# Causal masks of three attentions: from bf16 matmuls into PSUM to a VectorE add-and-reduce that writes the scores to SBUF

## The chip, the cores and the metric

The kernel runs on one core of a Trainium2 chip. The metric is the device time of one execution in microseconds; the median of three executions of the kernel before is 2026.19 us.

## What is computed

One sequence of 256 tokens with 1024 features goes through two networks one after the other, all in float32. The first has two layers; each is a SwiGLU feed-forward network (width 2816), a hybrid mixer, and a second feed-forward network. The mixer holds a gated linear recurrence, a convolution branch, and a latent attention with 8 heads. The second network is a dilated attention with 16 heads and three groups, a feed-forward network, a "forgetting" attention with 16 heads, another feed-forward network and a final norm.

What the change touches is the middle of each of the three attentions, shown here for the latent one (`mla_branch` of the reference):

```python
sc = (jnp.einsum('bqhd,bkhd->bhqk', qn, k_nope, preferred_element_type=jnp.float32)
      + jnp.einsum('bqhr,bkr->bhqk', qp, k_pe, preferred_element_type=jnp.float32)) * scale
mask = key_idx[None, :] <= q_idx[:, None]
sc = jnp.where(mask, sc, jnp.finfo(jnp.float32).min)
p = jax.nn.softmax(sc, axis=-1).astype(v.dtype)
return jnp.einsum('bhqk,bkhd->bqhd', p, v)
```

The dilated attention masks each group with a band, the forgetting attention uses the causal mask again.

## The kernel before

All weights come from HBM as 326 slots of 128 x 2048 floats (1 MB each), through a ring of three buffers. For each slot SyncE issues the load into `raw`, ScalarE rounds it to `whi` (`split`, line 586), VectorE computes the rest `wlo` = raw - whi (line 1107), and TensorE multiplies three times: activations high by `whi`, high by `wlo`, low by `whi` (`use`, line 1946, and `down_block`, line 1997). A slot is 24 matmuls of 512 columns. The order of every engine's work is written out by hand; semaphores connect the engines, and each engine works its own list in order.

The three attentions lie between or inside these slots.

- **Latent attention** (`scores_of` in `mix`, lines 2275 and 2276; twice, once for each layer). 8 heads in four pairs. `scores_of(p)` runs four score products (two heads, two row blocks of 128 queries with 128 and 256 keys). VectorE takes row maxima (`largest`, line 1390), ScalarE does the exponentials (line 778) and a scaling (line 786), TensorE transposes the probabilities (`turn_p`, line 2285) and multiplies by V (`pv`, line 2297). Between these steps stand whole stretches of projections, and VectorE also runs the 31 taps of the convolution branch (`conv`, line 1330) and the biased projections (line 1341).
- **Dilated attention** (`dil`). 32 items in 16 pairs, each with 512 score columns: `scores_of` (lines 2412 and 2415) puts two items into two PSUM banks. `largest` (line 1581), `exp` (line 962), `normed` (lines 1593 and 1595), `turn_p` (line 2422), `pv` (line 2436). A pair's `turn_p` comes a slot and more after its scores.
- **Forgetting attention** (`attention`, used by `fox`). 16 heads, with nothing else on TensorE for most of it. In iteration `h` TensorE does the scores of head `h` (`qk`, lines 2121 and 2123), the products by V of head `h-4` (`pv`, line 2152) and the transpositions of head `h-2` (`turn_p`, line 2133). VectorE takes the maxima (line 1211), ScalarE the exponentials (line 656) and the copy of the transposed probabilities (line 647).

Every score product opens with a mask matmul: the stationary operand is the bf16 identity `identb`, the moving one a piece of the bf16 masks `maskb`; it writes the mask into PSUM, and the float32 score product adds to it. GpSimd makes `identb` and `maskb` at the start (`masks`, line 1903).

```python
pe.matmul(dst[:, cols], identb[:], masks[rb][:, cols], start=True, stop=False)            # 2121
signal(dve.reduce_max(negmax[...], scores(groups, h, rb), AX, negate=True), max_done, ...)  # 1211
act.wait_ge(max_done, item(b, groups, h, rb))                                             # 653
if h >= h0 + 2:
    act.wait_ge(p_turned, item(b, groups, h - 2, rb))
act.activation(p_rows[h % 2][rb], scores(groups, h, rb), ACT.Exp, bias=negmax[...], accum_out=den[...])
```

`p_rows` are two SBUF buffers (heads `h % 2`), so ScalarE waits until TensorE has transposed head `h-2` before it writes head `h` there. `qk(h)` waits for `exp_done` of head `h-2`, `turn_p(h-2)` for `exp_done` of `h-2` and the copy of `h-4`, `pv(h-4)` for the copy of `h-4`. On ScalarE the order is exponentials of `h`, copy of `h-2`. VectorE also has `o_out` after head 11 (lines 1199 and 1204).

Of the kernel before, what the change touches and what calls it, by code (L numbers as in the profile page):

```python
# [26 lines left out]
AX = mybir.AxisListType.X  # L27
# [190 lines left out]
def program(nc, w_stream, gains, vecs, gate_w, chunks, b_f, fins, consts, x_in, positions, out):  # L218
    ctx = ExitStack()
    with ctx:  # L220
# [17 lines left out]
        identb = sb("identb", [P, P], BF16)  # L238
        maskb = sb("maskb", [P, 2 * P + RB * W], BF16)
# [14 lines left out]
        ident = con_("ident")  # L254
# [54 lines left out]
        d_p = [region(8960 + W * n, W) for n in range(2)]  # L309
# [28 lines left out]
        masks_done, trig_act, trig_pool = sem("masks_done"), sem("trig_act"), sem("trig_pool")  # L338
# [240 lines left out]
        def _(act):  # L579
# [57 lines left out]
            def attention(b, heads, h0, groups, p_rows, p_cols, tail=lambda h: None):  # L637

                lag = buffers(groups)
# [83 lines left out]
            def mix(b):  # L723
# [48 lines left out]
                def exp(p):  # L772
                    for h in (2 * p, 2 * p + 1):
                        act.wait_ge(mla_max, M * MH + h + 1)
                        if p:
                            act.wait_ge(mla_turned, M * MH + h - 1)
                        for rb in range(RB):
                            ins = act.activation(pm[h % 2][rb], mla_scores(h, rb), ACT.Exp, bias=negmax[:, 2 * h + rb:2 * h + rb + 1],
                                                 accum_out=den[:, rb * NH + h:rb * NH + h + 1])
# [144 lines left out]
            def dil(b):  # L924
# [33 lines left out]
                def exp(i):  # L958
                    act.wait_ge(max_done, b.head * 2 + i + 1)
                    if i >= 2:  # L960
                        act.wait_ge(p_turned, b.head * 2 + i - 1)
                    act.activation(d_p[i % 2], bank(dil_bank(i)), ACT.Exp, bias=negmax[:, i:i + 1],
# [49 lines left out]
            def fox(b):  # L1012
# [48 lines left out]
                attention(b, NH, 0, 1, x_p, x_pt, tail=lambda h: first_o(h - (NH - 2)))  # L1061
# [38 lines left out]
        def _(dve):  # L1100
# [37 lines left out]

            def copy_turn(b, plan, name, dst, parts):
# [42 lines left out]
            def attention(b, heads, h0, groups, p_cols, o_rows, more=lambda h: None):  # L1182
# [1620 lines left out]
```

## Time and profile before

| | |
|---|---|
| timed executions | 2026.12, 2026.19, 2026.45 us |
| profiled execution, first to last instruction (span) | 2024.2 us |
| TensorE matmul busy | 2001.7 us (99%) |
| TensorE weight load busy | 1649.0 us (81%) |
| VectorE busy | 1221.0 us (60%) |
| ScalarE busy | 1025.0 us (51%) |
| GpSimd busy | 284.7 us (14%) |
| mask matmuls recorded | 81 (32 latent, 17 dilated, 32 forgetting), with 96 loads of `identb` |

The page gives the profiled execution's span and no separate time for it; the timed median stands 2.0 us above the span, which is what lies around the first and last instruction. Matmuls are pipelined and their ends are modelled, so that their durations overlap: what one costs is the distance from its start to the next start, or its length in the chain of work. Some matmul records are missing: of the dilated attention's 32 mask matmuls 17 have one, while all 32 loads of the identity do.

### The profile page before, as it was taken

The page shows a single profiled execution, that of the slowest core. Times are in us where ns is not written, and L with a number is a line of the kernel's source. Part 1 is how long each engine was busy: PE and PEld are TensorE (multiplying, and loading weights), DVE is VectorE, ACT ScalarE, POOL GpSimd, SP SyncE. Part 2 cuts the span into 40 slices and gives each one's busy share as a digit, 9 for nine tenths or more (in the row PEclk, how much of TensorE's full clock was granted, in tenths as well). Part 3 has the DMA queues.
Part 4 walks back from the last instruction along what each step waited for, and adds up shares of the span by engine and source line. Part 5 has one row for each costly group of instructions (what it writes and reads, how often), then busy time and mean ns, then how long its engine had stood idle before and what let it go on. Part 6 is the DMA issues. An engine that isn't in the chain of part 4 may idle for free.

```text
span 2024.2 us, 26360 instructions
## 1 busy us (share of the span) xinstructions
PE 2001.7 (99%) x9813; PEld 1649.0 (81%) x9828; DVE 1221.0 (60%) x1374; ACT 1025.0 (51%) x1318; POOL 284.7 (14%) x365
## 2 busy tenths in 40 slices
PE   8999999999999999999999999999999999999998
PEld 6888888788888888887788888787778888788886
DVE  5555798865555555898855555555555555545554
ACT  5444685744445445586654445544444445455443
POOL 1000469200000000568100002111100000000000
PEclk9999999999999999999999999999999999999999
DMA  7554554445555554554455544344335554415552
GB/s 269 195 186 173 178 199 168 173 178 187 186 187 200 186 186 178 172 211 165 175 179 197 189 173 169 144 146 142 129 125 193 188 188 174 171 65 200 188 189 96
DMA packets 54626, 354.15 MB, mean 175 GB/s; under 512 B 7696, under 2 KB 8336, under 8 KB 12816
## 3 DMA queue, kind: packets, MB, share of 16 engines
q1 hardware_dynamic: 53968, 352.51, 49.1%
q8 instruction: 53, 0.87, 0.2%
q10 hardware_dynamic: 576, 0.53, 0.1%
q14 instruction: 29, 0.24, 0.0%
HBM read 351.97 MB, written 1.05 MB: 174 GB/s over the span
## 4 chain that ended last, share of the span: by engine, by line
PE 91%; DVE 5%; ACT 2%; issue 1%; DVEq 1%; DMA 0%; SPq 0%; POOLq 0%; ACTq 0%; POOL 0%
PE psum L1946 64%; PE psum L1997 18%; DVE wlo L1107 3%; PE psum L2075 2%; PE psum L2012 1%; PE psum L2415 1%; PE psum L2436 1%; PE psum L1958 1%; PE psum L2422 1%; ACT whi L586 1%; PE psum L2123 0%; PE psum L2152 0%; DMA raw<-w_stream 0%; DVE psum L1330 0%; PE psum L2276 0%
## 5 line engine op out<-in xcount | busy, mean ns | idle before, releaser
L1107 DVE TENSOR_TENSOR wlo<-raw,whi 128x2048 fp32r<-128x2048 f32 x325 | 752.0, 2317 | 388.5 <-ACT whi L586 386.0
L1946 PE MATMUL psum<-whi,xTh 128*128 128x512 f32 (+1 forms) x1920 | 764.3, 398 | 2.5 <-DVE xTl L1124 1.8
L1946 PE MATMUL psum<-whi,xTl 128*128 128x512 f32 (+1 forms) x1920 | 745.9, 388 | 0.0
L1946 PE MATMUL psum<-wlo,xTh 128*128 128x512 f32 (+1 forms) x1920 | 745.7, 388 | 0.0
L586 ACT ACTIVATE whi<-raw 128x2048 fp32r<-128x2048 f32 x325 | 622.0, 1916 | 239.8 <-PE psum L1997 151.3
L1946 PEld LDWEIGHTS psum<-whi,xTh 128*128 128x128 f32 x1920 | 361.2, 188 | 79.5 <-issue 7.1
L1946 PEld LDWEIGHTS psum<-whi,xTl 128*128 128x128 f32 x1920 | 361.1, 188 | 76.0
L1946 PEld LDWEIGHTS psum<-wlo,xTh 128*128 128x128 f32 x1920 | 361.7, 188 | 68.1
L1997 PE MATMUL psum<-whi,braT 128*128 128x512 f32 x1056 | 337.8, 390 | 0.0
L1997 PEld LDWEIGHTS psum<-whi,braT 128*128 128x128 f32 x1056 | 198.2, 188 | 41.2
L1997 PE MATMUL psum<-wlo,braT 128*128 128x512 f32 x528 | 205.5, 389 | 0.0
L683 ACT ACTIVATE arena<-psum,small 128x256 f32<-128x256 f32 x132 | 55.4, 471 | 194.8 <-PE psum L1946 194.7
L688 ACT ACTIVATE braT<-psum 128x256 fp32r<-128x256 f32 x132 | 43.4, 382 | 217.3 <-PE psum L2012 217.3
L1250 DVE TENSOR_TENSOR braT<-psum,braT 128x256 fp32r<-128x256 f32 x132 | 49.9, 420 | 112.1 <-ACT braT L688 112.1
L1997 PEld LDWEIGHTS psum<-wlo,braT 128*128 128x128 f32 x528 | 99.1, 188 | 20.0
L1243 DVE SCALAR_TENSOR_TENSOR arena<-psum,small,arena 128x256 f32<-128x256 f32 x132 | 57.8, 480 | 85.0 <-ACT arena L683 84.6
L1794 POOL TENSOR_SCALAR arena<-arena,vec 128x256 f32<-128x256 f32 x60 | 83.9, 1399 | 0.3 <-issue 0.3
L1330 DVE SCALAR_TENSOR_TENSOR psum<-arena,vec,psum 128x256 f32<-128x256 f32 x174 | 73.8, 485 | 5.4 <-issue 0.4
L1743 POOL TENSOR_SCALAR small<-small 128x2 f32<-128x2 f32 x9 | 1.7, 191 | 502.0 <-ACT arena L613 502.0
L1797 POOL TENSOR_TENSOR arena<-arena 128x256 f32<-128x256 f32 x60 | 68.0, 1134 | 8.8
L605 ACT ACTIVATE xTh<-psum,gain 128x256 fp32r<-128x256 f32 x80 | 31.3, 474 | 63.0 <-PE psum L1958 62.5
L1946 PE MATMUL psum<-whi,braT 128*128 128x512 f32 x160 | 56.0, 410 | 2.1 <-issue 2.1
(260 smaller groups left out, 1467.6 us busy)
## 6 DMA issues: line engine op xcount, KB each, us to landing
raw<-w_stream SPq DMA_DIRECT2D x326, 1024.0 KB, 4.8
bias<-chunks SPq DMA_DIRECT2D x18, 256.0 KB, 5.1
x<-x_in SPq DMA_DIRECT2D x2, 512.0 KB, 5.6
raw<-w_stream SPq DMA_DIRECT2D x4, 256.0 KB, 7.1
arena<-gate_w SPq DMA_DIRECT2D x2, 512.0 KB, 5.2
arena<-fins SPq DMA_DIRECT2D x2, 512.0 KB, 5.5
con<-consts SPq DMA_DIRECT2D x1, 720.0 KB, 10.8
out<-x ACTq DMA_DIRECT2D x2, 256.0 KB, 2.3
```

What stands on the lines that cost most here:

```text
L586: act.activation(whi[:, r], raw[:, r], ACT.Copy).then_inc(hi_done, 1)
L683: act.activation(f_sg[:, rb], gate_up(b, j)[:, rb, 0:256], ACT.Silu, scale=rs[:, rb:rb + 1]).then_inc(silu_done, 1)
L688: act.activation(h_of(b, j, 0)[:, :, rb * P:(rb + 1) * P], psum[:, 6 + rb, 0:256].rearrange("p (t s) -> p t s", s=P), ACT.Copy).then_inc(t ...
L1107: TT(wlo[:, r], raw[:, r], whi[:, r].bitcast(F32), ALU.subtract).then_inc(lo_done, 1)
L1243: ins = STT(f_h[:, rb], gate_up(b, j)[:, rb, 256:512], rs[:, rb:rb + 1], f_sg[:, rb], ALU.mult, ALU.mult)
L1250: TT(h_of(b, j, 1)[:, :, rows], psum[:, 6 + rb, 0:256].rearrange("p (t s) -> p t s", s=P), h_of(b, j, 0)[:, :, rows].bitcast(F32), ALU.sub ...
L1330: ins = STT(cacc[:, t] if k == TAPS - 1 else acc, cpad[:, t, k:k + S], w, acc, ALU.mult, ALU.add)
L1794: TS(ctap[:, k % 2], window, w, None, ALU.mult)
L1797: ins = TT(cacc[:, CONV_DVE], cacc[:, CONV_DVE], ctap[:, k % 2], ALU.add)
L1946: ins = pe.matmul(dst(rb), s(kt)[:, rows], w[:, r, at_:at_ + cols], start=start and n == 0 and k == 0, stop=stop and n == len(kts) - 1 and ...
L1997: ins = pe.matmul(pair(c)[:, rb], s[:, t, rows], w[:, r, t * D + c * W:t * D + (c + 1) * W], start=start and t == 0 and k == 0, stop=stop ...
L2075: ins = pe.transpose(dst[0:rows.shape[1], col:col + P], rows, ident)
```

## The change

The mask matmuls go. VectorE's row maximum becomes `tensor_tensor_reduce`: it reads the scores from PSUM and the float32 mask from SBUF (`con`, where the constants lie already), writes (scores + mask) x -1 to the SBUF buffer of the probabilities, and reduces with a minimum, which gives the negated maximum. ScalarE's exponential then runs in place in SBUF with scale -1. The wait for the buffer moves from ScalarE to VectorE. The dilated attention gets four such buffers for two. `identb`, `maskb`, their semaphore and GpSimd's `masks` are dropped.

```diff
-        d_p = [region(8960 + W * n, W) for n in range(2)]
+        d_p = [region(at_, W) for at_ in (8960, 9472, 11008, 11520)]
...
                         act.wait_ge(max_done, item(b, groups, h, rb))
-                        if h >= h0 + 2:
-                            act.wait_ge(p_turned, item(b, groups, h - 2, rb))
-                        signal(act.activation(p_rows[h % 2][rb], scores(groups, h, rb), ACT.Exp, bias=negmax[:, 2 * h + rb:2 * h + rb + 1],
-                                              accum_out=den[:, rb * NH + h:rb * NH + h + 1]), exp_done, groups, rb)
+                        signal(act.activation(p_rows[h % 2][rb], p_rows[h % 2][rb], ACT.Exp, bias=negmax[:, 2 * h + rb:2 * h + rb + 1],
+                                              scale=-1.0, accum_out=den[:, rb * NH + h:rb * NH + h + 1]), exp_done, groups, rb)
...
+            def masked_max(rows, scores_, mask, at_):
+
+                return dve.tensor_tensor_reduce(rows, scores_, mask, -1.0, 3.0e38, ALU.add, ALU.min, negmax[:, at_:at_ + 1])
...
                         dve.wait_ge(s_in, item(b, groups, h, rb))
-                        signal(dve.reduce_max(negmax[:, 2 * h + rb:2 * h + rb + 1], scores(groups, h, rb), AX, negate=True),
-                               max_done, groups, rb)
+                        if h >= h0 + 2:
+                            dve.wait_ge(p_turned, item(b, groups, h - 2, rb))
+                        signal(masked_max(p_rows[h % 2][rb], scores(groups, h, rb), masks[rb], 2 * h + rb), max_done, groups, rb)
...
                         dve.wait_ge(mla_s, M * MH + h + 1)
+                        if p:
+                            dve.wait_ge(mla_turned, M * MH + h - 1)
                         for rb in range(RB):
-                            ins = dve.reduce_max(negmax[:, 2 * h + rb:2 * h + rb + 1], mla_scores(h, rb), AX, negate=True)
+                            ins = masked_max(pm[h % 2][rb], mla_scores(h, rb), causal[:, (1 - rb) * P:2 * P], 2 * h + rb)
                         ins.then_inc(mla_max, 1)
...
                     dve.wait_ge(s_in, b.head * 2 + i + 1)
-                    dve.reduce_max(negmax[:, i:i + 1], bank(dil_bank(i)), AX, negate=True).then_inc(max_done, 1)
+                    if i >= 4:
+                        dve.wait_ge(p_turned, b.head * 2 + i - 3)
+                    blk = dil_item(i)[1]
+                    masked_max(d_p[i % 4], bank(dil_bank(i)), con_("mask_d")[:, blk * W:(blk + 1) * W], i).then_inc(max_done, 1)
...
-                        pe.matmul(dst[:, cols], identb[:], masks[rb][:, cols], start=True, stop=False)
                         for g in gs:
                             ins = pe.matmul(dst[:, g * keys:(g + 1) * keys], q_of(h, g)[:, rb * P:(rb + 1) * P],
-                                            k_of(h, g)[:, 0:keys], start=False, stop=g == gs[-1])
+                                            k_of(h, g)[:, 0:keys], start=g == g0, stop=g == gs[-1])
...
-                                pe.matmul(dst, identb[:], maskb[:, (1 - rb) * P:2 * P], start=True, stop=False)
-                                ins = pe.matmul(dst, qT[0:QK, h, rb * P:(rb + 1) * P], kT[0:QK, h, 0:keys], start=False, stop=True)
+                                ins = pe.matmul(dst, qT[0:QK, h, rb * P:(rb + 1) * P], kT[0:QK, h, 0:keys], start=True, stop=True)
...
-                    for bank_ in banks:
-                        pe.matmul(bank_, identb[:], maskb[:, 2 * P + blk * W:2 * P + (blk + 1) * W], start=True, stop=False)
```

The order of the built program shows what the diff does not. VectorE, forgetting attention, the maxima of heads 3 and 4 among the calls before (`small` holds the maxima):

```order
L1211 TENSOR_REDUCE small<-psum 128x1 [waits scores_in_psum] x4
L1690 TENSOR_SCALAR arena<-psum,small 128x512 [waits slot_used]
L1690 TENSOR_SCALAR arena<-psum,small 128x512
L1211 TENSOR_REDUCE small<-psum 128x1 [waits scores_in_psum] x20
L1199 RECIPROCAL small<-small 128x8 [waits exp_done]
```

and the same place now (`arena` is the probabilities' buffer, `con` the mask):

```order
L1693 TENSOR_SCALAR arena<-psum,small 128x512
L1133 ISA arena,small<-psum,con 128x128 [waits p_turned,scores_in_psum]
L1133 ISA small 128x1
L1133 ISA arena,small<-psum,con 128x256 [waits p_turned,scores_in_psum]
L1133 ISA small 128x1
L1133 ISA arena,small<-psum,con 128x128 [waits p_turned,scores_in_psum]
L1133 ISA small 128x1
```

Each maximum has become two instructions, the second of which only writes the 128 x 1 result, and from head 2 on they also wait for `p_turned`. VectorE's list has 96 such pairs for 96 reductions.

TensorE, one iteration of the forgetting attention before:

```order
L2121 MATMUL psum<-maskb,identb 128x128 [waits exp_done]
L2123 MATMUL psum<-arena 128x128
L2152 MATMUL psum<-arena 128x64 [waits pt_out_act]
L2121 MATMUL psum<-maskb,identb 128x256 [waits exp_done]
L2123 MATMUL psum<-arena 128x256
L2152 MATMUL psum<-arena 128x64 [waits pt_out_act]
L2152 MATMUL psum<-arena 128x64
L2133 MATMUL psum<-con,arena 128x128 [waits pt_out_act,exp_done] x2
L2133 MATMUL psum<-con,arena 128x128
```

Now the two rows of line 2121 are gone, the score products carry the wait for `exp_done`, and nothing else moved. The lists of ScalarE and SyncE keep their order; GpSimd's loses its two copies.

## Rows read from the trace of the kernel before

**Rows 1.** The page: busy time by engine; the chain that ended last.

```profile
PE 2001.7 (99%) x9813; PEld 1649.0 (81%) x9828; DVE 1221.0 (60%) x1374; ACT 1025.0 (51%) x1318; POOL 284.7 (14%) x365
...
PE 91%; DVE 5%; ACT 2%; issue 1%; DVEq 1%; DMA 0%; SPq 0%; POOLq 0%; ACTq 0%; POOL 0%
```

**Rows 2.** Chain, dilated attention, the mask matmuls of one pair: start us, us, what.

```profile
1265.84 0.07 issue
1265.91 0.38 PE psum L2412
```

**Rows 3.** Timeline, one pair: last normalization, first transposition (start, us, engine, line).

```profile
1331.15 0.49 DVE L1595 TENSOR_SCALAR arena<-arena,small 128x512 f32<-128x512 f32 x1
...
1336.41 0.27 PE L2422 MATMUL psum<-con,arena 128*128 128x128 f32 x1
```

**Rows 4.** Chain, mix stage of the first layer: where it leaves and rejoins TensorE.

```profile
348.21 0.62 DVE small L1390 x2
...
384.71 5.74 PE psum L1946 x24
```

**Rows 5.** Chain, forgetting attention, one head.

```profile
1787.00 0.06 PE psum L2121
1787.06 0.28 PE psum L2123 x2
1787.34 0.17 PE psum L2152 x2
1787.51 0.11 PE psum L2121
1787.62 0.43 PE psum L2123 x2
1788.05 0.39 PE psum L2152 x4
1788.44 0.34 PE psum L2133 x3
```

**Rows 6.** Timeline, the same stretch: VectorE's maxima, the next head's mask, ScalarE's exponential.

```profile
1786.31 0.62 DVE L1211 TENSOR_REDUCE small<-psum 128x1 f32<-128x128 f32 x2 [1.15 <-PE psum L2123]
...
1786.84 0.22 PE L2121 MATMUL psum<-maskb,identb 128*128 128x128 bf16 x1
...
1787.10 0.37 ACT L656 ACTIVATE arena<-psum,small 128x128 f32<-128x128 f32 x1 [0.48 <-PE psum L2133]
```

**Rows 7.** Timeline, the first heads: exponentials, copy, and TensorE behind them.

```profile
1780.34 0.37 ACT L656 ACTIVATE arena<-psum,small 128x128 f32<-128x128 f32 x1 [2.63 <-DVE small L1211]
...
1781.06 0.20 ACT L656 ACTIVATION_READ_ACCUMULATOR arena<-psum,small 128x1 f32 x1
1781.15 0.49 ACT L647 ACTIVATE arena<-psum 128x384 f32<-128x384 f32 x1
...
1781.31 0.23 PE L2121 MATMUL psum<-maskb,identb 128*128 128x128 bf16 x1 [0.55 <-ACT arena L656]
...
1781.78 0.41 PE L2152 MATMUL psum<-arena 128*128 128x64 f32 x2
```

**Rows 8.** Groups by line and shape: busy us, mean ns of one, idle before.

```profile
L1211 DVE TENSOR_REDUCE small<-psum 128x1 f32<-128x256 f32 x16 | 6.6, 415 | 0.0
L1250 DVE TENSOR_TENSOR braT<-psum,braT 128x256 fp32r<-128x256 f32 x132 | 49.9, 420 | 112.1 <-ACT braT L688 112.1
L1133 DVE TENSOR_TENSOR xTl<-psum,xTh 128x512 fp32r<-128x512 f32 x12 | 7.8, 684 | 8.2 <-ACT xTh L631 8.2
L778 ACT ACTIVATE arena<-psum,small 128x256 f32<-128x256 f32 x16 | 7.5, 471 | 0.0
L786 ACT ACTIVATE arena<-arena,small 128x256 f32<-128x256 f32 x16 | 7.9, 494 | 0.0
```

**Rows 9.** Timeline, end of the dilated attention: TensorE's longest wait there.

```profile
1477.76 0.47 PE L1946 MATMUL psum<-whi,braT 128*128 128x512 f32 x1 [2.14 <-issue]
```

**Rows 10.** Busy us by engine (TensorE, weight load, VectorE, ScalarE, GpSimd), granted clock, DMA.

```profile
1400.00:1500.00 100.00, 97.45 (x582) 76.72 (x587) 56.52 (x78) 45.68 (x72) 11.76 (x36) 0.98 0.35 125
```

More of the change, by code:

```diff
@@ L252, in vec_ @@
             return vec[:, VEC[n][0] + i:VEC[n][0] + i + m]
-        ident = con_("ident")
+        ident, causal = con_("ident"), con_("mask_s")
         at = [0]
@@ L635, in hi_turns, with attention @@
                     ins.then_inc(thi, 1)
-            def attention(b, heads, h0, groups, p_rows, p_cols, tail=lambda h: None):
-                lag = buffers(groups)
+            def attention(b, heads, h0, p_rows, p_cols, tail=lambda h: None):
+                groups, lag = 1, buffers(1)
                 def turned_out(h):
@@ L959, in exp @@
                     act.wait_ge(max_done, b.head * 2 + i + 1)
-                    if i >= 2:
-                        act.wait_ge(p_turned, b.head * 2 + i - 1)
-                    act.activation(d_p[i % 2], bank(dil_bank(i)), ACT.Exp, bias=negmax[:, i:i + 1],
+                    act.activation(d_p[i % 4], d_p[i % 4], ACT.Exp, bias=negmax[:, i:i + 1], scale=-1.0,
                                    accum_out=den[:, i:i + 1]).then_inc(exp_done, 1)
@@ L1060, in fox @@
                 first_o = lambda n: hi_turns(b, plan, f"o{n}", xTh[:, 2 * n:2 * n + 2], at_=4 + n)
-                attention(b, NH, 0, 1, x_p, x_pt, tail=lambda h: first_o(h - (NH - 2)))
+                attention(b, NH, 0, x_p, x_pt, tail=lambda h: first_o(h - (NH - 2)))
                 upto(13)
@@ L1180, in next_norm, with attention @@
                     norm_lo(b.next, 0)
-            def attention(b, heads, h0, groups, p_cols, o_rows, more=lambda h: None):
+            def attention(b, heads, h0, groups, p_rows, p_cols, o_rows, masks, more=lambda h: None):
                 lag = buffers(groups)
@@ L1402, in o_lo @@
                     TT(latT[:, 1, p], psum[:, 6, 0:S], latT[:, 0, p].bitcast(F32), ALU.subtract).then_inc(mla_lo, 1)
+                dve.wait_ge(rest_in, 48)
                 dve.wait_ge(vec_in, M * 16 + 16)
@@ L1594, in normed @@
                     dve.drain()
[L1595 removed]
+                    TS(d_p[i % 4], d_p[i % 4], rden[:, i:i + 1], None, ALU.mult).then_inc(p_normed, 1)
                 def o_lo(first):
@@ L1701, in more @@
                             lo_turns(b, plan, f"o{n}", xTl[:, 2 * n:2 * n + 2], xTh[:, 2 * n:2 * n + 2], at_=4 + n)
-                attention(b, NH, 0, 1, x_pt, x_o, more=more)
+                attention(b, NH, 0, 1, x_p, x_pt, x_o, (causal[:, P:2 * P], causal), more=more)
                 for n in range(2, 4):
@@ L1902, in _ @@
             TS(ang[:, 1], ang[:, 1], -1.0, np.pi / 2, ALU.mult, ALU.add).then_inc(trig_pool, 1)
-            def masks():
-                wait(rest_in, 48)
-                pool.tensor_copy(identb[:], ident)
-                m0 = CON["mask_s"][0]
-                pool.tensor_copy(maskb[:], con[:, m0:m0 + 2 * P + RB * W]).then_inc(masks_done, 1)
             def ffn(b):
                 rms(b)
-                if not b.early:
-                    masks()
             def fin(b):
@@ L2106, in whole, with attention @@
                         between()
-            def attention(b, heads, h0, groups, p_rows, p_cols, q_of, k_of, masks, v_of, before_pv=lambda: None):
+            def attention(b, heads, h0, groups, p_rows, p_cols, q_of, k_of, v_of, before_pv=lambda: None):
                 lag = buffers(groups)
@@ L2410, in scores_of @@
                     own = slice(blk * P, (blk + 1) * P)
-                    for bank_ in banks:
-                        pe.matmul(bank_, identb[:], maskb[:, 2 * P + blk * W:2 * P + (blk + 1) * W], start=True, stop=False)
                     for g, cols, keys in ((0, slice(0, S), slice(0, S)), (1, slice(S, S + P), own), (2, slice(S + P, W), own)):
                         for bank_, r in zip(banks, rows):
-                            ins = pe.matmul(bank_[:, cols], d_T[pair_ % 3][r, g, own], d_T[pair_ % 3][r, GROUPS + g][:, keys], start=False, stop=g == 2)
+                            ins = pe.matmul(bank_[:, cols], d_T[pair_ % 3][r, g, own], d_T[pair_ % 3][r, GROUPS + g][:, keys], start=g == 0, stop=g == 2)
                             if g == 2:
```

17 lines of the change are left out of this document (5 added, 12 removed).

## The prediction

> **What bounds the kernel.** I began with busy time by engine and then read the chain that ended last [rows 1]: TensorE is busy 99% of the span and 91% of the chain is its own work; the weight stream is nowhere in it (DMA 0%). So an instruction less on TensorE is worth its issue time, as long as no other engine's path is about to be the longer one. Three places decide, one for each attention, and the chain tells them apart. In the dilated attention every piece of the chain belongs to TensorE; the only other item is 0.07 us of issue in front of a pair's masks [rows 2]. In the forgetting attention the steady heads are TensorE's alone too, in seven pieces [rows 5]. In the mix stage it is not so: right after the third pair's scores the chain leaves TensorE for VectorE, passes through VectorE and ScalarE work, and comes back 36.5 us later [rows 4]. An average share would hide that.
>
> **The masks on TensorE.** 96 mask matmuls go, 32 in each attention. The dilated ones come in pairs (512 columns for each of two items); in the chain a pair and the gap in front are 0.07 + 0.38 = 0.45 us [rows 2]. 16 pairs x 0.45 = 7.2 us. The 0.38 us stand for both matmuls of a pair, of which mostly one has a record. The gap may stay when the 64-row score product follows the 128-row projection directly (0.38 us gained), or a second such gap behind the masks may close too (0.52 us): 6.1 to 8.3 us, and I take the middle. In the latent and the forgetting attention a head has a mask of 128 and one of 256 columns: 0.06 + 0.11 = 0.17 us [rows 5], so 16 x 0.17 = 2.7 us each if all of it were on the path.
>
> The Trainium skill ("TensorE: Matmul & The Clock Gate", Part 2) says that a weight load is pulled ahead of running matmuls when row groups do not conflict. By that rule the 64-row load behind a 128-row projection would wait for it, and the gap would stay: 6.1 us by the page against 7.2 by the row. No row shows that transition bare.
>
> **VectorE's new work.** A float32 two-input pass over 128x256 takes 420 ns where the reduction takes 415 [rows 8]: the same rate, one element a cycle, also with the result written. So the main instruction costs what the maximum did. New is the second instruction, which delivers the 128 x 1 result. VectorE's trace has none. From below it is nothing; from above it is the 0.20 us of ScalarE's accumulator read. Of that read ScalarE's next instruction waits only 0.09 us (1781.06 to 1781.15) [rows 7], and I take 0.09 us, as it is the same kind of step. A head's two maxima thus grow from 0.62 [rows 6] to 0.80 us.
>
> **ScalarE.** The exponential reads SBUF in place of PSUM: 494 against 471 ns for 128x256 [rows 8], 0.023 us more each, 0.05 us a head with the smaller one. Where ScalarE is not on the path this is free.
>
> **Dilated attention: all of it gained.** A pair has two maxima (two reads more, 0.2 us), two exponentials (0.05 us). They are covered: the last normalization ends at 1331.64 and the first transposition comes at 1336.41 [rows 3], 4.8 us of cover in which VectorE also splits a slot. Four buffers for two mean that the new wait for `p_turned` looks four items back, and is long past. -7.2 us.
>
> **Latent attention: nearly nothing.** Of the 2.7 us only the masks ahead of the point where the chain leaves TensorE count: two pairs and the start of the third, 0.34 x 2 + 0.17 = 0.85 us a layer. Behind it the chain is VectorE's, and its maxima are in it twice (third and fourth pair, 8 instructions): 8 x 0.09 = 0.7 us a layer more. The masks of the fourth pair lie beside it. Net 0.15 us a layer, and some 0.1 us more because VectorE now waits less for the third pair: -0.5 us for both layers. Bounds: -2.7 us if VectorE's wait absorbs its own growth, +1.5 us if the read costs the 0.20 us. What is late next there is the split of the slot at 384.7.
>
> **Forgetting attention: a new loop.** Here the moved wait matters. Before, VectorE took the maxima at once (1786.31) and only ScalarE waited for the transpositions of head h-2: these have been issued by 1786.84, the exponential starts at 1787.10, 0.26 us later [rows 6]. Now VectorE waits for them, and maxima and exponentials stand one behind the other. The loop over two heads, from the issue of `turn_p(h-2)` to that of `turn_p(h)`:
>
> - 0.26 us until VectorE starts [rows 6]; 0.80 us maxima; 0.05 us to ScalarE (TensorE starts 0.05 us after ScalarE's read ends at 1781.26 [rows 7]; I take the same).
> - Queued on ScalarE behind the exponentials of h is the copy for h-2, and `pv(h-2)` needs it before `turn_p(h)`. Exponential to copy 0.81 + 0.05, copy 0.49, to the product by V 0.14 (1781.64 to 1781.78) [rows 7]: 1.49 us.
> - TensorE from there: 0.17 + 0.43 + 0.39 + 0.34 = 1.33 us [rows 5].
>
> That is 3.93 us for two heads, 1.97 us a head, where the rows now sum to 0.06 + 0.28 + 0.17 + 0.11 + 0.43 + 0.39 + 0.34 = 1.78 us, with TensorE never idle. So each of the 12 heads 4 to 15 costs 0.19 us more, 2.2 us, in place of 0.17 us less. Added: once the division after head 11 (1.55 us on VectorE between two maxima that are 1.17 us apart) 0.4 us; the last head's chain, which is no longer hidden, 0.4 us; and back 0.3 us for the masks of the first two heads, which stand among projections. +2.7 us. Bounds: +1.3 us with a read that costs nothing and quick handovers, +4.5 us with the 0.20 us read.
>
> GpSimd's two copies at the start were hidden and nothing waited for them: 0.
>
> **Sum.** -7.2 - 0.5 + 2.7 = -5.0 us on a span of 2024.2 us. The timed median lies 2.0 us above the span, which the change does not touch: 2026.2 - 5.0 = 2021.2 us. The bounds of the three together give 2016.5 to 2025.7. One more term has no sign: TensorE waits 2.14 us at the end of the dilated attention [rows 9], and in that stretch the granted clock falls to 0.98 of full, that is 2% of 100 us, some 3.4 us at half of 2.4 GHz [rows 10]. Whether that recurs is worth up to 1.7 us either way.
>
> **Rivals.** About 0.2% (4.1 us) is what a measurement of this kernel can tell from no change.
>
> - *The loop stays hidden.* If handovers are short enough, all 96 masks are gained: -7.2 - 2.7 - 2.7 = -12.6, 2013.6 us. For it: TensorE never waits now. Against it: the sum above exceeds TensorE's 1.61 us a head by 0.36 us, more than any one term. Chance 0.06.
> - *The two-input reduction runs at half rate.* 256 further elements take 684 - 420 = 264 ns [rows 8], so a head's 384 elements cost 0.40 us more: the loop 0.20 us a head, 2.8 us with its ends; four heads a layer in the mix stage's chain, 3.2 us; the dilated attention's 1.1 us a pair is covered. -5.0 + 6.0 = +1.0, 2027.2 us. Against: plain two-input rows are at full rate. The Trainium skill ("Vector Engine (DVE) Microarchitecture Reference", section 7) says that an accumulating operation with two float32 SBUF sources halves its rate; here one source is PSUM, so by its letter it does not apply, and no row shows either. Chance 0.09.
> - *The dilated masks were partly cover.* If one of a pair's two masks hid the change from 128 to 64 rows, half of the 0.38 us comes back as a gap and a pair gains 0.19 us: 3.0 us in place of 7.2, which gives 2025.4 us. For it: a gap of 0.07 us already stands ahead of the masks [rows 2]. Against: nothing there waits for another engine. Chance 0.11.
> - *Slower: the new instruction has a large fixed cost.* Each x us more on one of them costs 14x in the forgetting attention (one x a head and its ends) and 16x in the mix stages. From x = 0.30 us on (30 x 0.30 = 9.1 us against 5.0 gained) the kernel is slower by over 4.1 us; at x = 0.5, 15 us: 2036 us. For it: the instruction's kind is nowhere in this trace. Against: every VectorE row with one pass is near its element count. Chance 0.06.
>
> **Numbers.** The forecast has 0.68, with a range of its own of 2018.5 to 2023.5; about three quarters of that lies below 2022.1, the rest within 0.2%. Faster: 0.52 + 0.06 = 0.58. Same: 0.16 + 0.09 + 0.11 = 0.36. Slower 0.06. The range for 8 in 10 leaves out the first rival, the last and half of the second: 2016.5 to 2026.5.
>
> **What would show it.** Right: no L2412, L2275 or L2121; in the dilated attention a pair's period shorter by 0.4 to 0.5 us; in the forgetting attention the head's period up from 1.77 to 1.9 or 2.0 us, with TensorE idle before its scores for ScalarE, and VectorE idle for the transpositions (L2133) and no more for the scores; the mix stage within 1 us of its old length. Wrong: a period there at or below 1.77 us, a maximum of 128x512 that takes over 0.9 us, a dilated pair that gains less than 0.3 us, or new waits of TensorE for `wlo`.

## The result, and the profile after

The changed kernel is slower: 2032.94 us median (2031.52 to 2036.32, 6 runs) against 2026.17 us (2024.37 to 2026.45, 6 runs), a ratio of 1.0039 with a 95% interval of 1.0029 to 1.0049, or 6.8 us more. The forecast was 2021.2 us with a range that ended at 2026.5 us, so the result lies 6.4 us above its end. The profiled execution took 2033.63 us, with a span of 2031.7 us.

The page of the kernel after: busy time by engine (as [rows 1]) and the granted clock in 40 slices.

```profile
PE 2007.0 (99%) x9732; PEld 1659.7 (82%) x9732; DVE 1222.5 (60%) x1470; ACT 1028.2 (51%) x1318; POOL 282.6 (14%) x363
...
PEclk9999999999999999999999999999999999969999
```

TensorE has 96 matmuls less to do and is busy 5.3 us longer than before. The second row says why: one slice of the clock, about 50 us wide, is a 6 among nines. Busy time by engine in five stretches of the forgetting attention (the columns are those of [rows 10]) puts it in place:

```profile
1770.00:1780.00 10.00, 8.90 (x46) 7.95 (x44) 3.53 (x18) 4.89 (x20) 0.00 (x0) 0.71 0.13 55
1780.00:1790.00 10.00, 10.00 (x45) 9.46 (x45) 1.96 (x12) 4.50 (x17) 0.00 (x0) 0.50 0.00 1
1790.00:1800.00 10.00, 10.00 (x44) 9.46 (x43) 3.43 (x16) 4.08 (x15) 0.00 (x0) 0.50 0.00 0
1800.00:1810.00 10.00, 10.00 (x45) 9.46 (x45) 2.61 (x16) 4.08 (x15) 0.00 (x0) 0.50 0.01 2
1810.00:1820.00 10.00, 10.00 (x60) 8.98 (x60) 2.85 (x6) 5.17 (x10) 0.00 (x0) 0.91 0.01 2
```

For 30 us on end TensorE is never idle (10.00 of 10 us) and its granted clock is 0.50 of full, 1.2 GHz. The shortfall of the five rows, 0.29, 0.50 three times and 0.09 of 10 us, is that of 37.6 us at half clock. TensorE's waits (who waits for whom: us in total, times, longest) have one row in the attention:

```profile
PE psum L2115 <- ACT arena L652: 1.1, 1, 1.1
```

The chain that ended last, in the same place (start us, us, what), shows what surrounds that wait and the fall behind it:

```profile
1764.12 5.47 PE psum L1940 x24
1769.62 1.01 DVE arena L1693 x2
...
1770.94 0.28 DVE arena L1133
...
1771.92 0.69 ACT arena L652 x3
...
1772.65 0.49 PE psum L2115 x2
...
1774.50 0.65 PE psum L2125 x3
1775.14 0.43 PE psum L2115 x2
1775.57 0.32 PE psum L2144 x2
1775.89 0.96 PE psum L2115 x2
...
1778.24 0.43 PE psum L2115 x2
```

The projections end; VectorE scales the second half of V (L1693), takes the maxima of head 2 (L1133), ScalarE takes the exponentials (L652), and TensorE waits for them 1.1 us in front of the scores of head 4 (L2115). About 2 us after it starts again the three transpositions (L2125) take 0.65 us where they took 0.34 [rows 5], and a head then takes 3.10 us (1775.14 to 1778.24) where it took 1.77 us. This goes on through the last scores, which end at 1807.79; the clock is full again from 1811.7 us on (0.65 in the stretch from 1811 to 1812, 1.00 in the next), 2.8 us ahead of the output projection.

Everything ahead of the attention went as forecast or a little better. One pair of the dilated attention in the chain after (beside [rows 2]):

```profile
1262.71 1.58 PE psum L1940 x6
1264.30 1.08 PE psum L2403 x12
```

In the chain the scores (L2403) follow the projection (L1940) within 0.01 us. The ends of the pieces are modelled, so the starts have to be read beside it; the timeline of the same pair, before and after (start us, us):

```profile
1265.45 0.39 PE L1946 MATMUL psum<-whi,xTl 128*128 128x512 f32 x1
1265.68 0.12 PEld L2412 LDWEIGHTS psum<-maskb,identb 128*128 128x128 bf16 x2 [0.27 <-issue]
1265.91 0.38 PE L2412 MATMUL psum<-maskb,identb 128*128 128x512 bf16 x1
1266.22 1.15 PE L2415 MATMUL psum<-arena 64*128 64x256 f32 x12
```

```profile
1263.91 0.39 PE L1940 MATMUL psum<-whi,xTl 128*128 128x512 f32 x1
1264.23 0.96 PEld L2403 LDWEIGHTS psum<-arena 64*128 64x128 f32 x12 [0.36 <-issue]
1264.23 1.15 PE L2403 MATMUL psum<-arena 64*128 64x256 f32 x12
```

From the start of the last projection to that of the scores it is 0.32 us where it was 0.77: 0.45 us gained. One projection follows another after 0.23 us, so 0.09 us still stand in front of the 64-row scores, as they did behind the masks before (1265.91 to 1266.22 is 0.31 us). By the same transitions in both chains, the stretch with the dilated attention goes from 483.57 us (1030.37 to 1513.94) to 476.46 us (1029.23 to 1505.69), 7.1 us less, and the 1.1 us between 1030.37 and 1029.23 are the gain of the two latent layers. The last transition ahead of the forgetting attention's projections for V is 8.28 us earlier (1760.17 before, 1751.89 after). When the projections for V end, the kernel after is 8.75 us ahead (1769.59 against 1778.34 in the chain before). It enters the output projection at 1814.51 where the kernel before did at 1807.35.

The new instructions, first by line and shape (busy us, mean ns | idle before), then as one line's instructions (shortest, median and longest ns, first and last start):

```profile
L1133 DVE CUSTOM_DVE_ANT_0 arena<-psum,con 128x256 f32<-128x256 f32 x32 | 13.4, 420 | 0.0
```

```profile
L1133 DVE DVE_READ_ACCUMULATOR2_ANT small<- x96: 75/82/85, 319.1 to 1809.9; 128x1 f32 x96
```

420 ns against 415 for the plain maximum of the same shape [rows 8]: full rate. And the second instruction, 82 ns long, costs nothing in a row of them: in the timeline of the run with four buffers below (start us, us; its line numbers are the same) the next one starts when the read starts, not when it ends:

```profile
1766.68 0.28 DVE L1133 CUSTOM_DVE_ANT_0 arena<-psum,con 128x128 f32<-128x128 f32 x1
...
1766.89 0.08 DVE L1133 DVE_READ_ACCUMULATOR2_ANT small<- 128x1 f32 x1
1766.89 0.42 DVE L1133 CUSTOM_DVE_ANT_0 arena<-psum,con 128x256 f32<-128x256 f32 x1
```

So the whole loss, and more, lies in 16 heads of one attention: from the end of the projections for V to the output projection 29.01 us before, 44.92 us after.

### The profile page after: what moved, and what is told of

The parts are those of the page before. It is cut to its first block, busy times and chain, and to the rows that moved or that the text cites. A ratio compares the mean times of both kernels' runs of the same rounds, so it can differ in the third digit from the quotient of the medians.

```text
span 2031.7 us, 26290 instructions
## 1 busy us (share of the span) xinstructions
PE 2007.0 (99%) x9732; PEld 1659.7 (82%) x9732; DVE 1222.5 (60%) x1470; ACT 1028.2 (51%) x1318; POOL 282.6 (14%) x363
## 4 chain that ended last, share of the span: by engine, by line
PE 89%; DVE 7%; ACT 2%; DVEq 1%; issue 1%; DMA 0%; SPq 0%; POOLq 0%; ACTq 0%
PE psum L1940 62%; PE psum L1991 18%; DVE wlo L1099 3%; PE psum L2069 1%; PE psum L2006 1%; DVE psum L1327 1%; PE psum L2115 1%; PE psum L2403 1%; PE psum L2424 1%; PE psum L1952 1%; PE psum L2144 1%; PE psum L2410 1%; ACT whi L584 1%; DVEq L1319 1%; DMA raw<-w_stream 0%
## 5 line engine op out<-in xcount | busy, mean ns | idle before, releaser
L1940 PE MATMUL psum<-whi,xTh 128*128 128x512 f32 (+1 forms) x1920 | 763.9, 398 | 4.1 <-DVE xTl L1116 3.4
L1940 PE MATMUL psum<-whi,xTl 128*128 128x512 f32 (+1 forms) x1920 | 745.5, 388 | 0.0
L1940 PE MATMUL psum<-wlo,xTh 128*128 128x512 f32 (+1 forms) x1920 | 745.4, 388 | 0.0
L1940 PEld LDWEIGHTS psum<-whi,xTh 128*128 128x128 f32 x1920 | 361.1, 188 | 80.8 <-issue 7.1
L1940 PEld LDWEIGHTS psum<-whi,xTl 128*128 128x128 f32 x1920 | 360.9, 188 | 75.9
L1940 PEld LDWEIGHTS psum<-wlo,xTh 128*128 128x128 f32 x1920 | 361.6, 188 | 68.1
L1991 PE MATMUL psum<-whi,braT 128*128 128x512 f32 x1056 | 337.8, 390 | 0.0
L1133 DVE CUSTOM_DVE_ANT_0 arena<-psum,con 128x128 f32<-128x128 f32 (+1 forms) x96 | 40.6, 465 | 53.1 <-PE psum L2125 28.2
```

Of the source, the lines that this page charges most:

```text
L1133: return dve.tensor_tensor_reduce(rows, scores_, mask, -1.0, 3.0e38, ALU.add, ALU.min, negmax[:, at_:at_ + 1])
L1940: ins = pe.matmul(dst(rb), s(kt)[:, rows], w[:, r, at_:at_ + cols], start=start and n == 0 and k == 0, stop=stop and n == len(kts) - 1 and ...
L1991: ins = pe.matmul(pair(c)[:, rb], s[:, t, rows], w[:, r, t * D + c * W:t * D + (c + 1) * W], start=start and t == 0 and k == 0, stop=stop ...
```

## The experiments

**First question: why does the clock fall?** Two theories at first. *Theory 1, content:* without the mask matmuls TensorE does too little there for the full clock. *Theory 2, wait:* VectorE now waits for the transpositions of two heads before, that delay reaches TensorE, and a microsecond of idleness drops the clock. The first four runs take the parts of the change in the forgetting attention apart: all of them back, only the mask matmuls back, only the wait away, only the mask matmuls away. In the expectations a "head period" is the time from one head's scores to the next one's, and "clock" is the mean over the span.

**The old forgetting attention with the rest of the change.**

```diff
-  signal(masked_max(p_rows[h % 2][rb], scores(groups, h, rb), masks[rb], 2 * h + rb), max_done, groups, rb)
+  signal(dve.reduce_max(negmax[:, 2 * h + rb:2 * h + rb + 1], scores(groups, h, rb), AX, negate=True), max_done, groups, rb)
...
+  pe.matmul(dst[:, cols], identb[:], masks[rb][:, cols], start=True, stop=False)
```

> The change in the dilated attention and the latent layers alone; the forgetting attention is as in the kernel before (masks by TensorE, plain row maximum, exponential out of PSUM). Both theories put the whole loss into the forgetting attention, so both expect 2026.2 - 7.2 (dilated attention) - 1.0 (two stages of the latent layers) = 2018.0 us, a head period of 1.77 us in the forgetting attention and a mean clock of 0.998. More than 2022 us would mean that a part of the loss comes from elsewhere.

Measured 2017.71 us (2017.05 to 2018.09), ratio 0.996 (0.9946 to 0.9974). The rest of the change is worth the 8.2 us that the anchors above gave, and the loss is the forgetting attention's alone.

**Masks added twice, by TensorE and by VectorE; two buffers and the moved wait stay.**

```diff
+  pe.matmul(dst[:, cols], identb[:], masks[rb][:, cols], start=True, stop=False)
   for g in gs:
       ins = pe.matmul(dst[:, g * keys:(g + 1) * keys], q_of(h, g)[:, rb * P:(rb + 1) * P],
-                      k_of(h, g)[:, 0:keys], start=g == g0, stop=g == gs[-1])
+                      k_of(h, g)[:, 0:keys], start=False, stop=g == gs[-1])
```

> The changed kernel with the mask matmuls of the forgetting attention back on TensorE, so that this mask is added twice, by TensorE and by VectorE. The moved wait on the turned exponentials stays. Theory 1 (content: without the mask matmuls TensorE does too little there for the full clock): the clock stays at 2.4 GHz, head period 1.85 to 1.95 us, 2019 to 2022 us. Theory 2 (wait: the idle microsecond from the moved wait drops the clock, whatever TensorE computes): the clock still falls to 1.2 GHz for over 30 us, head period about 3.1 us, 2033 us or more.

Measured 2019.57 us (2019.04 to 2021.41), ratio 0.9973 (0.9962 to 0.9983), clock 0.998 or 0.999 in all 8 runs. The moved wait is there and costs its time (two heads from 1771.86 to 1775.87 in its chain, 4.0 us), but the clock does not fall. TensorE's first wait in this run is 0.7 us.

**Four buffers, no masks.** VectorE waits for the turn of head h-4.

```diff
-  x_p = [[region(14464 + 384 * b + 128 * rb, (rb + 1) * P) for rb in range(RB)] for b in range(2)]
+  x_p = [[region(at_ + 128 * rb, (rb + 1) * P) for rb in range(RB)] for at_ in (14464, 14848, 18624, 19008)]
...
-  if h >= h0 + 2:
-      dve.wait_ge(p_turned, item(b, groups, h - 2, rb))
+  if h >= h0 + 4:
+      dve.wait_ge(p_turned, item(b, groups, h - 4, rb))
```

> The changed kernel with four buffers for the exponentials of the forgetting attention instead of two, so that VectorE waits for the turn of four heads before and not of two. The mask matmuls stay away. Theory 1 (content): the clock still falls, head period about 3.1 us, 2033 us. Theory 2 (wait): the clock stays at 2.4 GHz, TensorE is the bound at 1.6 to 1.7 us a head, 2015 to 2018 us.

Measured 2033.11 us (2031.65 to 2036.54), ratio 1.0038 (1.0024 to 1.0052): as slow as the change itself. Without the moved wait the clock falls all the same. Its waits have the same row as the change: 1.1 us, once.

**The kernel before without its mask matmuls in the forgetting attention.** It leaves out that attention's causal mask.

```diff
-  pe.matmul(dst[:, cols], identb[:], masks[rb][:, cols], start=True, stop=False)
```

> The kernel before, with the mask matmuls of the forgetting attention taken out and nothing in their place: it leaves out the causal mask of that attention, and moves no wait. Theory 1 (content): the clock falls there, some 13 to 15 us more than the kernel before, about 2040 us. Theory 2 (wait): no fall, 26 heads lose the 0.11 us of mask matmuls each where TensorE is the bound, about 2023.5 us.

Measured 2042.14 us (2041.49 to 2044.67), ratio 1.0085 (1.0068 to 1.0102). 32 matmuls fewer, nothing added and nothing moved, and 16 us slower. (The expectation's other sum, "26 heads" of 0.11 us, should have been 16 heads of 0.17 us, 2.7 us; it leads to the same 2023.5.) One stretch, then the row of its waits:

```profile
1790.00:1800.00 10.00, 10.00 (x43) 9.39 (x43) 1.87 (x6) 4.61 (x20) 0.00 (x0) 0.50 0.01 2
```

```profile
PE psum L2122 <- ACT arena L656: 1.0, 1, 1.0
```

All four came out as theory 1 had it; theory 2 in the form of the moved wait is out. But the waits, read in each run's profiled execution, show something that neither theory names. The three kernels without masks there have a first wait of 1.0 to 1.1 us, the two runs with them 0.5 and 0.7 us, because the masks of heads 2 and 3 stand in front of that wait and fill it. That gives **theory 3**: the length of this one wait, at the change from the projections to the attention, decides, and afterwards nothing brings the clock back.

**Second question: content or first wait?** Four runs with four buffers, in which the number and the place of the mask matmuls vary. The diff is that for heads 0 to 3; for heads 4 to 15 and for every second head its first line has `h >= 4` and `h % 2 == 1`, and for all heads the matmul stands without a condition.

```diff
+  masked = h < 4
+  if masked:
+      pe.matmul(dst[:, cols], identb[:], masks[rb][:, cols], start=True, stop=False)
```

> Four buffers for the exponentials and the mask matmuls of the forgetting attention back on TensorE (mask added twice). If the 1.9 us by which the run with masks twice and two buffers is above the run with the old forgetting attention (2019.6 against 2017.7) are the new loop through the buffers, they go: clock full, head period 1.77 us throughout, 2017.0 to 2018.3 us. If they are VectorE's longer maximum or ScalarE's longer exponential, it stays at 2019 to 2020 us.

> Four buffers; the mask matmuls on TensorE again, but only from head 4 on (heads 0 to 3 without). In all three runs that lost the clock, TensorE had waited 1.0 to 1.1 us for the first exponential just before. Theory 1 (content): the clock may fall in heads 0 to 3, and comes back within the attention once the masks are there: 2018 to 2025 us. Theory 3 (the longer first wait drops the clock and nothing in the attention brings it back): half clock until the output projection, 30 us or more, 2033 to 2038 us.

> Four buffers; the mask matmuls on TensorE again, but only for heads 0 to 3 (heads 4 to 15 without). Theory 1 (content): the clock is full through the first four heads and falls behind them, so the stretch at half clock is some 5 to 8 us shorter than the 37 us of the changed kernel: 2028 to 2031 us. Theory 3 (the longer first wait): with the first wait short again the clock never falls: 2015 to 2017 us.

> Four buffers; mask matmuls on TensorE for every second head of the forgetting attention. If half of them is enough for the full clock, this beats both kernels: 2017.7 less half of 16 x 0.17 us, 2016.3 us. If not, half clock for 35 us or more, 2032 to 2036 us.

Measured, with the first wait of the profiled execution:

| mask matmuls in | us, median | ratio, 95% | first wait | clock fell |
|---|---|---|---|---|
| all heads | 2018.13 | 0.9963 (0.995 to 0.9976) | 0.6 us | 0 of 5 |
| heads 0 to 3 | 2016.68 | 0.9954 (0.994 to 0.9968) | 0.6 us | 0 of 4 |
| every second head | 2015.53 to 2017.30; 2034.34 to 2039.35 | | 0.9 us | 3 of 12 |
| heads 4 to 15 | 2015.94 to 2018.09; 2037.01 to 2040.60 | | 1.1 us | 5 of 10 |

The third and fourth are two kernels each: in an execution the clock either falls (mean 0.986 to 0.989) or does not (0.998 or 0.999), so both groups are given and no median. Each group lies near what was expected with and without a fall; that one kernel would do both was in no expectation. The second row of the table refutes theory 1: twelve heads without a mask matmul run at full clock, 2016.7 us where theory 1 wanted 2028 to 2031. One of these heads in its chain, and the start of the next:

```profile
1775.70 0.22 PE psum L2130 x2
1775.93 0.17 PE psum L2159 x2
1776.10 0.49 PE psum L2130 x2
1776.59 0.39 PE psum L2159 x4
1776.98 0.34 PE psum L2140 x3
1777.31 0.22 PE psum L2130 x2
```

1.61 us a head, the sum of TensorE's own pieces, and no wait. The last row of the table shows the other half. Where the clock fell in heads 0 to 3, the masks that follow from head 4 on do not bring it back (the profiled execution, 0.50 in every stretch from 1775 to 1815 us), which speaks against theory 1 as well. That half of the executions escape there, where none did in the kernels with the same wait and no masks at all, shows that 1.1 us of waiting does not decide alone. With four buffers, all masks and no fall the run is 2.6 us below the one with two buffers when both stand at 0.999 (2016.7 against 2019.0 to 2019.6): 12 heads of 0.2 us, the price of the loop.

**Third question: the first wait by itself.** Four runs that change it in both directions. (a) All mask matmuls on TensorE, first wait longer:

```diff
+  TS(x_v[:, rb, W:W + 256], pair(units.place("v1"))[:, rb, 0:256], rs[:, rb:rb + 1], None, ALU.mult)
+  dve.drain()
```

> The run with the old forgetting attention (2017.7 us), where all mask matmuls are on TensorE, plus one VectorE pass over 128x256 (0.42 us) and a drain ahead of the maxima of head 2, so that TensorE's first wait in the attention grows from 0.55 to about 1.0 us. Theory 3 (the length of this first wait decides): the clock falls although all masks are there, in all or in some runs, and stays low through 14 heads: 2034 to 2042 us where it does. Theory 1 (content): no fall, 2018.2 us.

Measured 2037.49 us (2036.37 to 2037.66), ratio 1.0058 (1.0042 to 1.0073), the clock at 0.988 or 0.989 in all 4 runs: 19.8 us slower than the same kernel without the one VectorE pass and the drain, although every mask matmul is there. Its first wait, and two stretches from there on:

```profile
PE psum L2130 <- ACT arena L656: 1.1, 1, 1.1
```

```profile
1770.00:1780.00 10.00, 8.89 (x48) 7.97 (x47) 3.10 (x10) 5.07 (x20) 0.00 (x0) 0.70 0.02 6
1780.00:1790.00 10.00, 10.00 (x46) 9.27 (x46) 1.87 (x6) 3.88 (x15) 0.00 (x0) 0.50 0.00 1
```

(b) No mask matmul in any head, four buffers, first wait filled with products that nobody reads:

```diff
+  if h == h0 + 4:
+      units_left(b, units, "v0")
+      for _ in range(8):
+          pe.matmul(psum[:, 0, 0:2 * P], identb[:], maskb[:, 0:2 * P], start=True, stop=True)
```

> Four buffers, no mask matmul in any head, but eight products of 128 x 256 columns in bfloat16 whose result nobody reads, right where TensorE waits 1.1 us for the first exponential. Theory 3: TensorE is busy there, the clock stays full through 14 heads without masks at 1.61 us a head: 2017.7 less 16 x 0.17 us is 2015.0 us. Theory 1 (content, at least in the first heads): half clock for over 30 us, 2031 to 2034 us.

Measured 2014.78 us (2014.11 to 2016.37), ratio 0.9946 (0.9932 to 0.9959), no fall in 5 runs. Of the wait 0.2 us is left, and the stretch that ran at 0.50 in the run with four buffers alone is at full clock:

```profile
PE psum L2126 <- ACT arena L654: 0.2, 1, 0.2
```

```profile
1780.00:1790.00 10.00, 10.00 (x82) 9.46 (x80) 5.24 (x28) 8.26 (x32) 0.00 (x0) 1.00 0.01 2
```

(c) The changed kernel itself, two buffers, with the same eight products:

> The changed kernel (two buffers, no mask matmul) with the same eight products in the first wait. Theory 3: full clock; what is left is the loop through two buffers, about 1.9 us a head against 1.77: 2018 to 2020.5 us, which is what the forecast of 2021.2 us meant. Theory 1, or theory 2 (waits of the loop are enough to drop the clock when no masks are there): half clock, 2031 to 2034 us.

Measured 2019.10 us (2018.22 to 2020.27), ratio 0.9969 (0.9956 to 0.9981), no fall in 6 runs. Eight products that nobody reads make the changed kernel 13.8 us faster. What is left is the loop. TensorE's waits in the attention, then its chain from the end of one head's transpositions to that of the next but one:

```profile
PE psum L2126 <- ACT arena L654: 1.5, 6, 0.3
PE psum L2155 <- ACT arena L647: 0.6, 1, 0.6
```

```profile
1773.31 0.03 issue
...
1773.45 0.14 DVE arena L1135
...
1774.44 0.69 ACT arena L654 x3
...
1775.17 0.49 PE psum L2126 x2
...
1776.86 0.35 PE psum L2136 x3
1777.21 0.03 issue
```

(d) No filling product: VectorE scales the second half of V behind the maxima of head 2 instead of ahead of them.

```diff
-  if h == 1:
+  if h == 2:
       v_out(1)
```

> Four buffers, no mask matmul and no filling product; instead VectorE scales the second half of V (1.4 us) behind the maxima of head 2 and not ahead of them, so that TensorE's first wait of 1.1 us becomes two of about 0.4 us. Theory 3 in its narrow form (one long wait decides): full clock, 2015 us. If the sum of the waits there counts, or theory 1 holds: the clock falls in all or in some runs, 2031 us and more there.

Measured 2015.33 us (2013.64 to 2017.51), ratio 0.9951 (0.9936 to 0.9967), no fall in 4 runs. The wait for the exponential is 0.4 us:

```profile
PE psum L2115 <- ACT arena L652: 0.4, 1, 0.4
```

The expectation spoke of two waits of 0.4 us; the trace has one and no other in the attention, so this run does not tell one long wait from the same idle time in two pieces. Run (c) says something on that: its seven waits sum to 2.1 us, none longer than 0.6, and the clock stays.

So it is shown from both sides that this one wait matters: longer, it drops the clock with all masks in place; shorter or filled, it does not with none. (b) and (d) beat both kernels by more than 10 us; their intervals overlap, so which of them is better is open. Open too is how the odds depend on the wait: 0.9 us lost the clock in 3 of 12 executions, 1.1 us in 5 of 10 where masks followed from head 4 on, and in 19 of 19 in the other four kernels with 1.0 or 1.1 us.

The length of a wait does not decide by itself, and the traces have a second place that says so. At the end of the dilated attention TensorE waits about twice as long [rows 9], in the profiled execution of each of the 14 kernels, with large projections behind the wait. Here the change and the run with the old forgetting attention (the columns of [rows 10]; then the product behind the wait):

```profile
1465.00:1485.00 20.00, 17.82 (x99) 13.78 (x98) 10.65 (x19) 6.41 (x10) 1.34 (x6) 0.91 0.30 109
1465.00:1485.00 20.00, 17.82 (x108) 13.97 (x107) 11.63 (x20) 7.53 (x13) 1.35 (x6) 1.00 0.34 118
```

```profile
1470.45 0.76 PE L1940 MATMUL psum<-whi,braT 128*128 128x512 f32 x1 [2.18 <-issue]
1470.91 0.47 PE L1952 MATMUL psum<-whi,braT 128*128 128x512 f32 x1 [2.18 <-issue]
```

With the same 2.18 us of waiting the clock falls in one and not in the other. It falls in 7 of the 14 profiled executions, and in the change it is back after some 3.4 us at half speed (0.69, 0.50, 0.50 and 0.61 in the four microseconds from 1470 on), where in the forgetting attention it takes 37.6 us. So 1.1 us is no threshold to carry elsewhere; the size of the products around the wait may have a part in it, and no run here takes that apart.

## Why the prediction was wrong

By its own terms:

- **Dilated attention, -7.2 us:** 7.1 us measured in the stage. The choice to count the gap in front of the masks with them gave the right 0.45 us a pair, and the 4.8 us of cover hid the rest. But the 0.07 us was not a gap: it belongs to the pair's first mask, which has no record (its load starts at 1265.68, 0.23 us behind the last projection). The real gap of 0.09 us stood between the masks and the scores, and stands in front of the scores still. The Trainium skill ("TensorE: Matmul & The Clock Gate", Part 2) says that a load is pulled ahead when the row groups do not conflict, and the trace agrees with what was drawn from it: the 64-row load is not pulled ahead, it starts with its product at 1264.23. The 128-row loads of the projections start 0.23 us ahead of their product (1263.68 for the one at 1263.91); the page names a second case beside the row groups, a load into the background weight buffer, which the prediction left out. What failed was to take 6.1 us from the rule, since that gap was there before the change too.
- **Latent layers, -0.5 us:** 1.1 us less measured. The term for the second instruction, 0.09 us each, was too large: it costs nothing in a row. Two maxima of a head take 0.63 us (1766.68 to 1767.31 in the timeline above), not 0.80. With it at nothing the prediction's own terms would give 1.9 us, so the gain of the masks was sized too high: in the first layer the second pair's scores take 1.57 us in the chain after (330.57 to 332.14) where they took 1.77 (330.66 to 332.43), 0.20 of the expected 0.34 us. That layer is 0.71 us ahead when its chain comes back to TensorE (384.00 against 384.71).
- **The rivals:** half rate and a large fixed cost are out by 420 against 415 ns, partly covering dilated masks by the 7.1 us, a hidden loop by the 3.90 us below.
- **Forgetting attention, +2.7 us: the step that failed.** As measured the term is +15.4 us (44.92 - 29.01, less the 0.47 us below). With the clock held by filling, the term is +1.9 us: from the end of the projections for V to the output projection 31.41 us (1768.16 to 1799.57 in the chain of (c)) against 29.01, less the 0.47 us (8.75 - 8.28) that the projections with the first heads' masks gained. That lies within its bounds of 1.3 to 4.5 us. The loop's length came out, 3.90 us for two heads (1773.31 to 1777.21) against 3.93, but not by the path that was summed, and that the sums agree is luck. The prediction went from the exponentials over ScalarE's copy to the product by V. In (c) the chain goes from the exponentials (L654) straight to the next scores (L2126), six waits against one for the copy (L647). The 0.26 us in front of the maxima are 0.14 (1773.31 to 1773.45), their 0.80 are 0.66 (to 1774.11), and TensorE's share is its whole 2.04 us (1775.17 to 1777.21) and not 1.33. Of the 0.8 us between +2.7 and +1.9, two thirds of a microsecond have a place: head 11 ran free of the loop (1.62 us, 1784.99 to 1786.61, where 1.97 was counted), head 4 cost 0.03 us and not 0.19 (5.15 us from the end of the projections against 5.12), and the first heads' masks gave 0.47 back and not 0.3. So at full clock the forecast of 2021.2 us stands against 2019.1 us.

What the term left out, and what made the whole forecast fail, is the clock: it put the clock's part at nothing, and the change without and with the filling products differs by 13.8 us. Every duration of TensorE in that term was taken at 2.4 GHz, and the only sentence on the clock ("One more term has no sign") looked at the end of the dilated attention, where it had already fallen once. It did not ask where else TensorE comes close to such a fall, and the row was there: [rows 7] has TensorE waiting 0.55 us in front of the scores of head 4, right behind the projections, and the mask row beside it. The mask matmuls ahead of that wait were priced as time on the path, a gain of 0.17 us a head. But in front of a wait for another engine they are cover. The chain through VectorE and ScalarE is as long as before (2.97 us from 1778.34 to 1781.31, then 3.06 us from 1769.59 to 1772.65), so every mask that goes there turns into idleness: 0.34 us for the four masks and 0.09 us from the longer chain are 0.43 of the 0.54 us by which the wait grew, from 0.55 to 1.09 us (the other 0.1 us has no row of its own). That costs no time by itself; it cost half of the clock for 37.6 us. In numbers: 13.8 us between the change and (c), where the loop hides behind the slower TensorE (the run with two and the one with four buffers take 44.92 and 44.91 us from V to the output projection), and 18.3 us between four buffers alone and (b), where there is no loop.

The rival for "slower" named an expensive instruction, and no instruction was expensive. A rival "the clock falls where the projections give way to the attention" was missing; its price could have been worked out from rows: TensorE's own 1.61 us a head once more, for up to 14 heads. The sum of the bounds has a slip as well: -6.1 + 1.5 + 4.5 = -0.1 gives 2026.1 us at the upper end and not 2025.7; the range of 8 in 10 took that in, and the result lies outside either.

That a dip at the end of the dilated attention comes and goes held: the granted clock of that stretch is 0.98 in the profiled executions of the change and of (b), as in [rows 10], and 1.00 in those of the first run and of (c). Its worth of up to 1.7 us fits the times: in the run with masks twice and two buffers five executions at a mean clock of 0.999 took 2019.0 to 2019.6 us and three at 0.998 took 2020.8 to 2021.4. The times of the kernel before lie in two groups too, 2024.2 to 2025.1 and 2025.7 to 2026.6 us (one at 2027.75), but its mean clocks do not sort them, so there the link is not shown.

## What to carry to other kernels

In this kernel the work of TensorE in front of a wait for another engine was not only time, it was also what kept the engine busy at that point. Before taking such work away, look at how long the wait behind it becomes, and look first at places where small products follow the wait: here a longer wait with large projections behind it cost about 1.7 us or nothing, the shorter one ahead of the small products 14 to 20 us. If a change makes a TensorE-bound kernel slower although it removes TensorE work, read the granted clock in stretches before anything else. Two cheap remedies worked here: to reorder the waited-for engine's queue (here one line: scale V after the maxima) or to fill the wait with products that nobody reads.

## What was not expected of the hardware

- A single wait of 1.0 to 1.1 us behind projections with TensorE never idle was enough for a fall to 1.2 GHz in 24 of 29 executions of five kernels; waits of 0.2 to 0.7 us were not followed by one there (37 executions of seven variants, and all 46 of the kernel before that ran beside them). The waits are those of the profiled executions. A wait of 2.18 us ahead of large projections, at the end of the dilated attention, was followed by a fall in some profiled executions and not in others.
- Once fallen, the clock stayed at 0.50 through the whole attention although TensorE was busy 10.00 of 10 us; it came back at 1811.7 us, 3.9 us after the last score product, with only products by V and transpositions since. The Trainium skill ("TensorE: Matmul & The Clock Gate", Part 1) says that activity releases the throttle. Here 30 us of uninterrupted small products did not, so being busy in this trace's sense was not enough.
- At the same kernel and the same place the clock falls in one execution and not in the next: two sets of times 20 us apart, 2015.94 to 2018.09 and 2037.01 to 2040.60 us.
- At half clock a head's pieces are 0.43 + 0.32 + 0.96 + 0.75 + 0.64 = 3.10 us against 0.22 + 0.17 + 0.49 + 0.39 + 0.34 = 1.61 us, a factor of 1.92: nearly the whole time of a head goes with TensorE's clock.
- VectorE's next instruction starts with the 82-ns read of the accumulator; ScalarE's starts 0.09 us behind the start of its own read [rows 7].
